# A two-layer decoder trunk on one core: the sparse attention's outputs as three rounded products in a ring of two key blocks

## What is computed

```python
def dsa_mixer(hn, w_in, w_out, cos_a, sin_a, cos_i, sin_i):
    q, k, v, qi, ki, wi = jnp.split(hn @ w_in, _splits(OD_SIZES), axis=-1)
    ...
    def block(args):              # 128 queries
        ...
        score = jnp.where(kpos[None, None, :] <= tq[None, :, None], score, -jnp.inf)
        _, idx = lax.top_k(score, topk)          # 128 keys per query
        ...
        p = jax.nn.softmax(s, axis=-1).astype(v.dtype)
        o = jnp.einsum('bqkgn,bqnkd->bqkgd', p, v_sel)
        return o.reshape(Bsz, Q_BLOCK, ATT_HEADS * ATT_HEAD_DIM)
```

## Time and profile before

| | |
|---|---|
| median of three runs | 2190.7 us |
| the profiled execution | 2190.2 us |
| its span | 2188.4 us |
| granted clock of TensorE, mean | 0.999 |
| TensorE busy | 2173.3 us (99%) |
| VectorE busy | 1051.1 us (48%) |
| ScalarE busy | 452.5 us (21%) |
| GpSimd busy | 1538.1 us (70%) |

### The profile page before, as it was taken

How to read it: one execution, slowest core, us unless ns; L and a number is a source line. 1 busy time by engine, 2 the same in 40 slices (tenths; PEclk the granted TensorE clock), 3 DMA queues, 4 the chain that set the end, 5 groups by cost and what they waited for, 6 DMA issues and landing times. The chain is left out here.

```text
span 2188.4 us, 30358 instructions
## 1 busy us (share of the span) xinstructions
PE 2173.3 (99%) x10590; PEld 1797.1 (82%) x10590; DVE 1051.1 (48%) x1386; ACT 452.5 (21%) x808; POOL 1538.1 (70%) x1538
## 2 busy tenths in 40 slices
PE   9999999999999999999999999999999999999998
PEld 7888888888888888888888888886878888888887
DVE  6556795695444352233362224357872543222333
ACT  3101212034123210001131111134362332111112
POOL 7777787667974777776677777685756647777774
PEclk9999999999999999999999999999999999999999
DMA  5333333223331333333333333332322223333332
GB/s 193 96 96 115 115 96 122 87 78 97 125 97 53 101 96 96 96 98 97 112 98 98 96 98 96 96 101 76 103 87 92 78 63 96 96 96 97 98 97 82
DMA packets 115318, 214.11 MB, mean 98 GB/s; under 512 B 12816, under 2 KB 14368, under 8 KB 114976
## 3 DMA queue, kind: packets, MB, share of 16 engines
q1 hardware_dynamic: 111168, 202.16, 29.5%
q10 hardware_dynamic: 4064, 10.84, 1.5%
HBM read 208.76 MB, written 4.19 MB: 97 GB/s over the span
## 5 line engine op out<-in xcount | busy, mean ns | idle before, releaser
L426 PE MATMUL ps<-x,w_split 128*128 128x512 f32 (+1 forms) x2862 | 1109.1, 388 | 0.7 <-DVE x L2138 0.4
L428 PE MATMUL ps<-x,w_split 128*128 128x512 f32 (+1 forms) x2862 | 1100.4, 384 | 0.0
L427 PE MATMUL ps<-x,w_split 128*128 128x512 f32 (+1 forms) x2862 | 1100.3, 384 | 0.0
L391 POOL TENSOR_TENSOR w_split<-w_raw,w_split 128x512 fp32r<-128x512 f32 x758 | 1025.5, 1353 | 63.1
L387 POOL TENSOR_SCALAR w_split<-w_raw 128x512 fp32r<-128x512 f32 x758 | 502.5, 663 | 562.0 <-PE ps L428 559.6
L426 PEld LDWEIGHTS ps<-x,w_split 128*128 128x128 f32 x2862 | 537.9, 188 | 118.4 <-issue 9.7
L427 PEld LDWEIGHTS ps<-x,w_split 128*128 128x128 f32 x2862 | 538.0, 188 | 107.3 <-issue 1.4
L428 PEld LDWEIGHTS ps<-x,w_split 128*128 128x128 f32 x2862 | 537.8, 188 | 107.2
L1823 DVE TENSOR_TENSOR x<-arena,x 128x512 fp32r<-128x512 f32 x88 | 118.7, 1360 | 219.0 <-ACT x L1281 219.0
L1773 DVE TENSOR_TENSOR tu<-ps,rstd 128x512 f32<-128x512 f32 x88 | 60.7, 689 | 315.6 <-PE ps L428 315.6
L1219 ACT ACTIVATE sg<-tg 128x512 f32<-128x512 f32 x88 | 55.6, 632 | 669.2 <-DVE tg L1770 668.0
(11 more groups left out here) (297 smaller groups left out, 1327.8 us busy)
## 6 DMA issues: line engine op xcount, KB each, us to landing
w_raw<-in_stream SPq DMA_DIRECT2D x758, 256.0 KB, 2.6
arena<-in_memT ACTq DMA_DIRECT2D x2, 1024.0 KB, 5.2
s_tables<-kv ACTq DMA_DIRECT2D x4, 512.0 KB, 3.2
arena<-s_tables ACTq DMA_DIRECT2D x4, 512.0 KB, 4.5
out<-h ACTq DMA_DIRECT2D x6, 256.0 KB, 2.4
h<-in_xT SPq DMA_DIRECT2D x4, 256.0 KB, 5.2
h<-in_xT SPq DMA_DIRECT2D x2, 512.0 KB, 6.0
w_raw<-in_stream SPq DMA_DIRECT2D x6, 128.0 KB, 5.1
```

Source lines behind the costliest of these rows:

```text
L391: pool.tensor_tensor(W[:, s, 1, c], raw[:, s, c], W[:, s, 0, c].bitcast(F32), ALU.subtract).then_inc(split_ready if half else S("half_spli ...
L426: pe.matmul(dst, wh, xh, start=start, stop=False)
L427: pe.matmul(dst, wh, xl, start=False, stop=False)
L428: return pe.matmul(dst, wl, xh, start=False, stop=stop)
```

## The change

The value tensor (128x1024, two value heads of four key blocks) is split once, by ScalarE at the head of its attention and by VectorE behind the first front, into chunks 0 and 1 of `X[1]`, which are free once the last input projection is done. The turned weights of key block kc are split by ScalarE (in place of the copy) and VectorE (`turned_lower`, new) into chunk 2 + kc % 2 of `X[1]`: a ring of two key blocks. So units with more than two key blocks have their outputs in two parts, and the third block's parts may be written only when the first part's products have read the ring (`att_oh`). Each product of line 991 becomes three rounded ones. TensorE transposes into a PSUM bank only when VectorE, too, has read it (`att_tl` in place of `att_t`).

```diff
+        def split_od_val(part):
+            return X[1][:, part, :, :].rearrange("p a t -> p (a t)").rearrange("p (t d) -> p t d", t=4)
+        def split_turned(kc, part):
+            return X[1][:, 2 + kc % 2, part, :]
...
+                def outputs(i, kcs):
+                    g, qb = UNITS[i]
+                    if kcs[0] == 0:
+                        pe.wait_ge(*((S("x_lo"), X_LO_ATT + i) if i else (S("od_v_lo"), 1)))
+                    gc = slice(g * P, (g + 1) * P)
+                    done = UNIT_TR[i] - qb - 1
+                    for kc in kcs:
+                        pe.wait_ge(S("att_t"), done + kc + 1)
+                        for part in range(2):
+                            pe.matmul(ps[:, 0, :], split_od_val(part)[:, kc, gc], split_turned(kc, 0),
+                                      start=(kc == 0 and part == 0), stop=False)
+                    for kc in kcs:
+                        pe.wait_ge(S("att_tl"), done + kc + 1)
+                        m = pe.matmul(ps[:, 0, :], split_od_val(0)[:, kc, gc], split_turned(kc, 1),
+                                      start=False, stop=(kc == qb))
+                    m.then_inc(S("att_o") if kcs[-1] == qb else S("att_oh"), 1)
+
...
                         if kc == 2:
                             fill(1)
+                            outputs(i, (0, 1))
                         if nt >= 2:
-                            pe.wait_ge(S("att_t"), nt - 1)
+                            pe.wait_ge(S("att_tl"), nt - 1)
...
-                    if i == 0:
-                        pe.wait_ge(S("od_v"), 4)
-                    else:
-                        pe.wait_ge(S("x_lo"), X_LO_ATT + i)
-                    pe.wait_ge(S("att_t"), nt)
-                    for kc in range(qb + 1):
-                        m = pe.matmul(ps[:, 0, :], od_val[:, kc, g * P:(g + 1) * P],
-                                      area(A_PT + kc * T), start=(kc == 0), stop=(kc == qb))
-                    m.then_inc(S("att_o"), 1)
+                    outputs(i, range(2 if qb >= 2 else 0, qb + 1))
...
-                    act.activation(area(A_PT + kc * T), ps[:, 6 + nt % 2, :], ACT.Copy).then_inc(S("att_t"), 1)
-
+                    if kc == 2:
+                        act.wait_ge(S("att_oh"), sum(qb >= 2 for _, qb in UNITS[:i + 1]))
+                    act.activation(split_turned(kc, 0), ps[:, 6 + nt % 2, :], ACT.Copy).then_inc(S("att_t"), 1)
+
+                act.wait_ge(S("block_done"), od_block(OD_TILES - 1) + 1)
+                act.wait_ge(S("od_v"), 4)
+                act.activation(split_od_val(0), od_val, ACT.Copy).then_inc(S("od_v_hi"), 1)
                 act.activation(tiny[:, 0, 0:1], epsc[:, 0:1], ACT.Exp)
...
+                def turned_lower(i, kc):
+                    nt = UNIT_TR[i] - UNITS[i][1] - 1 + kc
+                    dve.wait_ge(S("att_t"), nt + 1)
+                    if i >= 1 and kc == 0:
+                        dve.wait_ge(S("att_o"), i)
+                    if kc == 2:
+                        dve.wait_ge(S("att_oh"), sum(qb >= 2 for _, qb in UNITS[:i + 1]))
+                    dve.tensor_tensor(split_turned(kc, 1), ps[:, 6 + nt % 2, :], split_turned(kc, 0).bitcast(F32),
+                                      ALU.subtract).then_inc(S("att_tl"), 1)
+
                 front(0)
-                dve.wait_ge(S("od_v"), 4)
+                dve.wait_ge(S("od_v_hi"), 1)
+                dve.tensor_tensor(split_od_val(1), od_val, split_od_val(0).bitcast(F32), ALU.subtract
+                                  ).then_inc(S("od_v_lo"), 1)
                 inverse(0)
                 front(1)
                 topk(5)
                 for i in range(len(UNITS)):
+                    for kc in range(min(2, UNITS[i][1] + 1)):
+                        turned_lower(i, kc)
                     topk([1, 2, 2, 4, 4, 0, 0, 0][i])
+                    for kc in range(2, UNITS[i][1] + 1):
+                        turned_lower(i, kc)
                     if i + 1 < len(UNITS):
                         inverse(i + 1)
                     topk([2, 3, 2, 4, 4, 0, 0, 0][i])
```

## The result

The changed kernel takes 2195.98 us (median of 15 runs, 2194.99 to 2197.45); the kernel before took 2190.59 us in 15 runs on the same chip (2190.1 to 2191.53). The ratio is 1.0025, 95% interval 1.0018 to 1.0032: 5.4 us slower. That is just over the 0.2% that the prediction drew as its bound, above its 2194.2 us and inside its range.

What follows compares the result with a forecast made beforehand. TensorE, busy 99% of the span, was taken as the bound. Its -3.6 us of work plus the new waits summed to +3.55 us on the 2190.7 us median: 2194.2 us, range 2190.5 to 2197.5.

Steps and rivals of the forecast that it cites:

- unit 4's last product: TensorE waits for unit 4's last subtraction, queued on VectorE behind top-k rounds: 1.8 us.
- unit 5's transpositions: TensorE waits for unit 5's scaling, whose reciprocal is queued behind unit 4's last subtraction: 2.1 us.
- the second fill: At attention's start, ScalarE's value rounding delays its first key copy, so the array resumes about 0.55 us late.
- The eight waits: New TensorE waits in attention: 0.55, 0.25, 0.2, 1.8, 2.1, 0.8, 1.1 and 0.35 us.
- step (c): Units 3 and 4: VectorE's queue delays unit 4's last subtraction, then unit 5's reciprocal; waits of 1.8 and 2.1 us.
- the likeliest case: The prediction's own case, 60%: 2194.2 us, within 0.2% of before, own range 2192.5 to 2196.
- The array's own work: TensorE at line 991: 17.2 us removed, 13.6 us of rounded products added, net -3.6 us.
- other units, so nothing: Remaining units: their 2.95 us fills cover one copy and one subtraction, so no wait.
- unit 5's lowering: TensorE's first fill in unit 5 ends before VectorE's lowering at 24.3: wait 0.8 us.
- The gain comes through: Rival, 10%: the VectorE walk is pessimistic, only the start's and unit 7's waits stay: 2188.0 us.
- The longer queue: Rival, 20%: in units 2 to 5 subtractions block VectorE longer and signals cost 0.1 us more: 2195.8 us.
- The clock falls: Rival, 8%: the 1.8 and 2.1 us waits lower TensorE's clock, +2.2 us per fill run so: 2197.5 us.

Runs made afterwards that it cites:

- e2: The changed kernel without the 33 top-k rounds that VectorE makes during attention: 2190.72 us.
- e4: The changed kernel without VectorE's 20 subtractions of turned weights, the third product reading the upper part again: 2191.5 us.
- e1: The changed kernel with ScalarE's split of the value tensor moved behind the table load and first copy of keys: 2194.07 us.
- e10: The kernel before, with unit 6's fill moved behind unit 4 and unit 7's exponentials ahead of that fill's copy: 2191.03 us.
- e12: e1 plus eight unused products of ones on TensorE in the wait ahead of unit 5: 2193.32 us.
- e5: The changed kernel with the value split later and VectorE's order rewritten, unit 5's reciprocal ahead of the third block's subtraction, rounds dealt anew: 2190.37 us.
- e8: The changed kernel with one fill moved from behind unit 6 to behind unit 4: 2196.09 us.
- e11: e8 plus ScalarE making unit 7's exponentials ahead of the moved fill's copy: 2192.11 us.

## Why the prediction came out as it did

**Its mechanism was right.** The waits stand where the walk put them: unit 4's last product 1.50 us for 1.8, unit 5's transpositions 2.08 for 2.1, unit 6 1.10 for 1.1, the second fill 0.57 for 0.55, unit 7 0.35 more for 0.35. The eight waits sum to 7.15 in the prediction and to 7.01 in the trace. The subtractions took 0.68 us each, the value tensor's lower part 2.32 us (3.5 forecast) and hid as forecast, VectorE's added work is 16.1 us (15 to 18 forecast), and nothing behind attention changed (534.2 us from the stretch's end to the span's in both). The two waits of step (c) make up half of it, and e2 and e4 show the two causes that step (c) named, a queue of rounds and a reciprocal behind a subtraction: for unit 5 either is enough without the other.

The size fell short: +3.55 us was forecast and +5.4 measured, so the likeliest case's "within 0.2%" (4.4 us) was missed, and the time lies at the upper end of that case's own range (2196). These make up the difference.

**The array's own work was mis-sized.** The prediction took 0.227 us for a rounded product. Four in a row take 1615.55 - 1614.62 = 0.93, or 0.2325 each; 60 make 13.95, so 3.25 us are saved rather than 3.6. (Unit 1, which waits for nothing, went from 10.82 to 10.67 us with one block, 0.15 a block; unit 6's two blocks between two fills went from 4.60 to 4.26, 0.17 a block: 3.0 to 3.4 for 20.)

**One wait was missed**, under "other units, so nothing": unit 3's last product, 0.25. And four in the sum were off, though they nearly cancel, which is luck: unit 0's 0.67 for 0.25, units 2 and 3's 0.36 for 0.2, unit 4's 1.50 for 1.8, unit 5's lowering 0.38 for 0.8. With these the sum is 7.01 + 0.25 - 3.25 = +4.01 us, and the stretch shows +4.27. The rows behind a wait are longer, which the sum left out: the four products at 1601.64 and at 1639.73 take 1.03 and 1.04 us until the next one starts, for 0.93 where nothing waited, and unit 0's last product 0.34 for 0.24.

**The rest is outside the stretch.** The medians are 5.4 us apart and the two profiled executions 4.8 (that of after is 1.0 below its median, that of before 0.4 below its own), of which 0.6 lie ahead of attention. Part may be the clock: in 8 of the 15 runs the mean granted clock was 0.997 or 0.998, with a mean time of 2196.4, in the other 7 it was 0.999, with 2195.6, which would make 0.4 us of the median at most. But a low mean doesn't tell where the clock was low. Runs of the kernel before have it too (7 of the 29 beside e1), and the profile of e10, with a mean of 0.997, has every low window at the two ends of the span, such as this one:

```profile
8.00:10.00 2.00, 1.31 (x3) 1.12 (x4) 1.68 (x2) 0.72 (x1) 1.92 (x3) 0.50 1.09 410
```

So what makes up the last 1.1 us stays open.

**The rivals.** "The gain comes through" fell with the first wait. "The longer queue" gave 2195.8, near the measured median, but not by its own price: the subtractions cost what the sum said. "The clock falls" was given 8%. The profiled run of after kept 1.00 through its two waits, and whether the clock fell there in others of its 15 runs is not shown; in e1's profile it did, at less than the rival's price (1.0 us, where the rival had 3.3). The argument against it, that the clock took some 5 us to fall at the span's end, was drawn from one place and doesn't hold here: in e1 the transpositions right behind the second wait (1633.48 to 1634.46) already take 0.98 us instead of 0.85. The Trainium skill (TensorE: Matmul & The Clock Gate, Why this matters for your kernels) advises against idle gaps between bursts of matmuls; e1 and e12, which differ in eight products in such a gap, point the same way. But each of the two gaps in e1 is shorter than those that the page names, so by its rule the clock would have stayed up; the measurement decides.

**What the prediction didn't see** is e4's finding: it priced each wait by the new subtractions, and the saving was lost without them too. It had the spare 0.7 us ahead of unit 5 and the six moved products in its own sum for (c), but didn't set one against the other. The moved products lowered the array's cover there (1.4 us) by more than the rounding did (1.1).

## What to carry to other kernels

When an engine that is busy 99% gets less to do, lay the other engines' queues beside it in that stretch and ask how much cover they lose; an engine busy 48% overall can be 0.8 us from the bound there, and everything over that becomes a wait. Count as lost cover what is moved ahead of a chain's beginning (here, products that a small ring forces early) together with what is saved. A step that nobody needs until later should not stand in a queue ahead of one on the path (the reciprocal behind the subtraction, the fill's copy ahead of the exponentials): with order, cover and placement changed together, the change that cost 5.4 us gained 2.5, and none of e1, e5, e8 and e11, which make one or two of these moves, was faster than before.

## What the hardware showed that I had not expected

**The clock can fall behind two short waits, or one.** In e1's profile it fell to 0.55 and 0.60 for two windows of 2 us, behind waits of 1.3 and 1.8 us with one product between. Products of 256 columns then start 0.21 us apart instead of 0.12, as in this piece of TensorE's timeline:

```profile
1635.04 0.41 PE L436 MATMUL ps<-w_split,x 128*128 128x256 f32 x1
1635.25 0.41 PE L434 MATMUL ps<-w_split,x 128*128 128x256 f32 x1
...
1637.85 0.28 PE L435 MATMUL ps<-w_split,x 128*128 128x256 f32 x1
1637.96 0.28 PE L436 MATMUL ps<-w_split,x 128*128 128x256 f32 x1
```

It stayed up behind a wait of 1.30 us alone (e12, e2) and fell behind one of 2.79 (e8); the pair of 1.3 and 1.8 has it down in e1's profile and up in that of after. Each of these is one profiled execution.

**A 128x4 operation on VectorE took up to 1.07 us.** Line 2380 negates four columns; its eight instructions take 0.171 to 1.072 us. Two of them beside GpSimd, in the timeline of the changed kernel:

```profile
1574.32 1.29 POOL L399 TENSOR_TENSOR w_split<-w_raw,w_split 128x512 fp32r<-128x512 f32 x1
...
1574.84 0.79 DVE L2380 TENSOR_SCALAR col<-col 128x4 f32<-128x4 f32 x1
```

```profile
1612.49 1.30 POOL L399 TENSOR_TENSOR w_split<-w_raw,w_split 128x512 fp32r<-128x512 f32 x1
...
1612.74 1.07 DVE L2380 TENSOR_SCALAR col<-col 128x4 f32<-128x4 f32 x1
```

Each ends 0.02 us behind GpSimd's operation (1575.63 and 1575.61, 1613.81 and 1613.79), as do the two others of the eight that take 0.46 and 0.58 us; the four of 0.17 or 0.18 us start within 0.2 us of a GpSimd operation's end or with none beside them. The Trainium skill (SBUF — State Buffer, SBUF: two separate sides) has a pair of ports that GpSimd shares with those VectorE operations that run in a two-port performance mode or have two SBUF inputs, and whichever engine came first holds it for its whole instruction. The rows agree, though no run shows the mode of line 2380. Unit 0's wait needs this beside the five rounds: in e1 the same operation took 0.17 us, a 128x512 operation behind it 0.61 in place of 0.81, and VectorE reached the subtraction that much earlier against the array, which then didn't wait; in e2 the operation took 0.79 us, and without the rounds nothing waited either. Between after and e1 the work is the same and only the phase between the two engines has moved, so a wait of 0.7 us can come or go with an edit elsewhere.
